# One opening block for two queues, and the last 128 columns for two other engines

## The reference, cut to what matters

```
h = concatenate([meta, x])
for i in range(2):
    a = rmsnorm(h, g[i][0])
    m = retention_mixer(a, ...) if i == 0 else rglru_mixer(a, ...)
    h = h + rmsnorm(m, g[i][1])
    f = conv_ffn(rmsnorm(h, g[i][2]), ...)
    h = h + rmsnorm(f, g[i][3])
return h[:, 16:]
```

## Time and profile before

| what | value |
|---|---|
| median of three runs | 696.47 us (696.41 to 696.52) |
| profiled execution | 696.7 us |
| its span, first to last instruction | 694.9 us |
| TensorE matmul busy | 688.1 us, 99% |
| VectorE busy | 618.9 us, 89% |
| ScalarE busy | 522.3 us, 75% |
| GpSimd busy | 25.2 us, 4% |
| memory read | 129.23 MB |

### The profile page before, as it was taken

One profiled execution on the slowest core, in us unless ns is written; L12 is line 12 of the kernel. 1 busy time (PEld: TensorE's weight loads), 2 busy tenths in 40 slices (PEclk: granted clock), 3 DMA queues, 4 the chain that ended last, 5 costly groups with the idle time before them and its releaser, 6 DMA issues.

```text
span 694.9 us, 15951 instructions
## 1 busy us (share of the span) xinstructions
PE 688.1 (99%) x6471; PEld 579.0 (83%) x6471; DVE 618.9 (89%) x868; ACT 522.3 (75%) x851; POOL 25.2 (4%) x26
## 2 busy tenths in 40 slices
PE   9999999999999999999999999999999999999997
PEld 7888888888999888888889998888888888884454
DVE  6989898978989799998998889999999999999533
ACT  7477867767755888987888677999878888897441
POOL 0002010100110000000003000000000000000000
PEclk9999999999999999999999999999999999999999
DMA  9875656462643455655589941110545656566821
GB/s 345 325 256 155 246 147 252 139 216 105 220 206 121 154 213 191 232 203 199 202 331 384 354 148 62 62 61 1 182 166 199 237 195 224 199 232 220 256 41 61
DMA packets 48635, 134.51 MB, mean 194 GB/s; under 512 B 30784, under 2 KB 31296, under 8 KB 33344
## 3 DMA queue, kind: packets, MB, share of 16 engines
q1 hardware_dynamic: 48288, 133.39, 54.8%
q10 hardware_dynamic: 288, 0.31, 0.1%
HBM read 129.23 MB, written 1.05 MB: 187 GB/s over the span
## 4 chain that ended last, share of the span: by engine, by line
PE 96%; DVE 2%; DMA 1%; issue 1%; ACT 0%; POOLq 0%; DVEq 0%; SPq 0%; ACTq 0%
PE ps L1894 25%; PE ps L1895 25%; PE ps L1896 25%; PE ps L2397 3%; PE ps L2395 3%; PE ps L2396 3%; PE ps L2329 1%; PE ps L1926 1%; PE ps L1947 1%; PE ps L1927 1%; PE ps L2042 1%; PE ps L2049 1%; PE ps L2044 1%; DMA stage<-in_chunks 1%; PE ps L2145 1%
## 5 line engine op out<-in xcount | busy, mean ns | idle before, releaser
L1894 PE MATMUL ps<-a_hi,w_hi 128*128 128x272 f16 (+1 forms) x1008 | 279.2, 277 | 0.2 <-DVE w_lo L1097 0.2
L1895 PE MATMUL ps<-a_lo,w_hi 128*128 128x272 f16 (+1 forms) x1008 | 279.1, 277 | 0.0
L1896 PE MATMUL ps<-a_hi,w_lo 128*128 128x272 f16 (+1 forms) x1008 | 279.1, 277 | 0.0
L1097 DVE SCALAR_TENSOR_TENSOR w_lo<-stage,w_hi 128x1024 f16<-128x1024 f32 x205 | 247.4, 1234 | 20.6 <-ACT w_hi L566 20.2
L566 ACT ACTIVATE w_hi<-stage 128x1024 f16<-128x1024 f32 x205 | 207.8, 1046 | 49.8 <-PE ps L2397 18.3
L1894 PEld LDWEIGHTS ps<-a_hi,w_hi 128*128 128x128 f16 x1008 | 98.6, 98 | 16.8 <-DVE w_lo L1097 0.5
L1896 PEld LDWEIGHTS ps<-a_hi,w_lo 128*128 128x128 f16 x1008 | 98.6, 98 | 16.1
L1895 PEld LDWEIGHTS ps<-a_lo,w_hi 128*128 128x128 f16 x1008 | 98.6, 98 | 16.0
L1894 PE MATMUL ps<-y_hi,w_hi 128*128 128x272 f16 (+3 forms) x496 | 106.1, 242 | 0.0
L1895 PE MATMUL ps<-y_lo,w_hi 128*128 128x272 f16 (+3 forms) x496 | 106.0, 242 | 0.0
L1896 PE MATMUL ps<-y_hi,w_lo 128*128 128x272 f16 (+3 forms) x496 | 106.0, 242 | 0.0
(11 more groups left out here) (320 smaller groups left out, 1074.9 us busy)
## 6 DMA issues: line engine op xcount, KB each, us to landing
stage<-in_chunks SPq DMA_DIRECT2D x118, 1024.0 KB
work<-work SPq DMA_DIRECT2D x96, 32.0 KB, 2.1
stage<-in_chunks SPq DMA_DIRECT2D x6, 256.0 KB
decay_all<-in_decay SPq DMA_DIRECT2D x1, 1056.0 KB, 11.9
out<-sq SPq DMA_DIRECT2D x4, 256.0 KB, 2.0
hT<-in_tokens SPq DMA_DIRECT2D x3, 272.0 KB, 5.5
stage<-in_chunks SPq DMA_DIRECT2D x1, 512.0 KB
mT<-in_gains SPq DMA_DIRECT2D x1, 512.0 KB, 6.7
```

The costliest lines, as they stand in the source:

```text
L1097: dve.scalar_tensor_tensor(out=part(1, c, q), in0=flat(stage, c, q), scalar=W_SCALE, in1=part(0, c, q), op0=ALU.mult, op1=ALU.subtract).th ...
L1894: pe.matmul(o, w_h, x_h, start=start, stop=False)
L1895: pe.matmul(o, w_h, x_l, start=False, stop=False)
L1896: return pe.matmul(o, w_l, x_h, start=False, stop=stop)
```

## The change: what it does

The opening: row 0 of the first chunk (512 columns), the 64 gain columns and token tile 0 (272 columns) now lie side by side in memory and in one SBUF region. Each partition has 848 columns of them, 424 KB in all. Partitions 0 to 63 are brought by SP's queue as its first transfer, partitions 64 to 127 by ACT's queue as its first. VectorE and ScalarE both wait for both halves (`x_landed[0]` at 32). SP's other transfers, and token tile 1 on ACT's queue, keep their order. The rotary table is put over the place where row 0 lay, so its transfer now waits until `w_lo` of row 0 has been made (`even_low`).

The end: for token tile 1, VectorE's second run of line 1809 covers 384 columns. The other 128 are scaled by ScalarE (a copy with the root as its scale, in place), once the root is made (`fin_root`), and GpSimd then adds `h_rows` (`fin_pool`). SyncE waits for `fin_pool` too ahead of the last transfer.

```diff
+OPENING = CW + 8 * DT + T
...
-        hT_all = sb("hT", [P, 8 * DT + DT * T])
-        hT = hT_all[:, 8 * DT:].rearrange("p (a b) -> p a b", b=T)
+        rope_first = sb("rope_first", [P, 2 * T - CW + OPENING + (DT - 1) * T])
+        rope_sb = rope_first[:, 0:2 * T].rearrange("p (a b) -> p a b", b=T)
+        hT_all = rope_first[:, 2 * T - CW:]
+        first_row = hT_all[:, 0:CW]
+        hT = hT_all[:, CW + 8 * DT:].rearrange("p (a b) -> p a b", b=T)
...
+        POOL_COLS = slice(2 * BANK - P, 2 * BANK)
...
             first_chunk = chunks[0:2 * P, :].rearrange("r n -> (r n)")
-            for k0, count in FIRST_ROWS:
+            sp.dma_start(hT_all[0:P // 2, 0:OPENING],
+                         tokens[0:P // 2 * OPENING].rearrange("(p n) -> p n", p=P // 2)).then_inc(x_landed[0], 16)
+            for k0, count in FIRST_ROWS[1:]:
...
                 if c == 1:
-                    sp.dma_start(rope_sb[:], rope).then_inc(table_landed, 16)
+                    sp.wait_ge(even_low, 1)
+                    sp.dma_start(rope_sb, rope).then_inc(table_landed, 16)
...
             for b in range(4):
                 sp.wait_ge(fin_out, b + 1)
+                if b == 3:
+                    sp.wait_ge(fin_pool, 1)
...
                     if dt < KC - 2:
-                        if dt in row_landed:
+                        if dt == 0:
+                            act.wait_ge(x_landed[0], 32)
+                        elif dt in row_landed:
                             act.wait_ge(row_landed[dt], 32)
...
-                        act.activation(w_hi[0][:, dt, :], stage[0][:, dt, :], ACTF.Copy,
+                        act.activation(w_hi[0][:, dt, :], stage[0][:, dt, :] if dt else first_row, ACTF.Copy,
...
-            for n, (a, b) in enumerate(((0, 8 * DT + T), (8 * DT + T, 8 * DT + 2 * T))):
-                act.dma_start(hT_all[:, a:b], tokens[P * a:P * b].rearrange("(p n) -> p n", p=P)).then_inc(x_landed[n], 16)
+            act.dma_start(hT_all[P // 2:P, 0:OPENING],
+                          tokens[P // 2 * OPENING:P * OPENING].rearrange("(p n) -> p n", p=P // 2)).then_inc(x_landed[0], 16)
+            act.dma_start(hT[:, 1, :], tokens[P * OPENING:P * (OPENING + T)].rearrange("(p n) -> p n",
+                                                                                       p=P)).then_inc(x_landed[1], 16)
...
+            act.wait_ge(fin_m, 5)
+            act.wait_ge(rows_landed, 32 * 16)
+            act.wait_ge(fin_root, 2)
+            act.activation(fin[:, 1, POOL_COLS], fin[:, 1, POOL_COLS], ACTF.Copy,
+                           scale=fin_s[:, 4, 1:2]).then_inc(fin_scaled, 1)
...
-            dve.wait_ge(x_landed[0], 16)
+            dve.wait_ge(x_landed[0], 32)
...
-                link(dve.scalar_tensor_tensor(out=r, in0=t_, scalar=3.0, in1=r0, op0=ALU.subtract, op1=ALU.mult))
+                dve.scalar_tensor_tensor(out=r, in0=t_, scalar=3.0, in1=r0, op0=ALU.subtract,
+                                         op1=ALU.mult).then_inc(fin_root, 1)
+                dve.wait_ge(fin_root, tt + 1)
                 dve.wait_ge(fin_m, n_sum)
                 for half in range(2):
-                    cols = slice(half * BANK, (half + 1) * BANK)
+                    cols = slice(half * BANK, POOL_COLS.start if half and tt else (half + 1) * BANK)
...
+            def final_columns():
+
+                pool.wait_ge(fin_scaled, 1)
+                pool.tensor_tensor(fin[:, 1, POOL_COLS], fin[:, 1, POOL_COLS], h_rows[:, 1, POOL_COLS],
+                                   ALU.add).then_inc(fin_pool, 1)
...
+            final_columns()
```

More of the change, by code:

```diff
@@ L179, in build @@
         ones_sb = sb("ones_sb", [P, P])
-        rope_sb = sb("rope_sb", [P, 2, T])
         decay_all = sb("decay_all", [P, 8 * T])
         decay_sb = decay_all[:, 0:HEADS * DECAY_W].rearrange("p (h j) -> p h j", j=DECAY_W)
-        gains_sb = hT_all[:, 0:8 * DT]
+        gains_sb = hT_all[:, CW:CW + 8 * DT]
         par = sb("par", [P, LRU_PARS])
@@ L333, in build @@
         x_landed = [sem(f"x_landed{j}") for j in range(len(TOKEN_LOADS))]
-        row_landed = {k: sem(f"row_landed{k}") for k in (0, 1, 2, 4, 5)}
+        row_landed = {k: sem(f"row_landed{k}") for k in (1, 2, 4, 5)}
         even_high = sem("even_high")
@@ L367, in build @@
         m_est = sem("m_est")
+        fin_root = sem("fin_root")
+        fin_scaled = sem("fin_scaled")
+        fin_pool = sem("fin_pool")
         rs_made = sem("rs_made")
@@ L480, in load_tokens @@
                 dt, count = TOKEN_LOADS[n]
-                at = P * (8 * DT + dt * T)
+                at = P * (OPENING + (dt - 1) * T)
                 sp.dma_start(hT[:, dt:dt + count, :].rearrange("p a b -> p (a b)"),
@@ L1328, in _ @@
                         dve.wait_ge(even_high, dt // 2 + 1)
-                    dve.scalar_tensor_tensor(out=w_lo[0][:, dt, :], in0=stage[0][:, dt, :], scalar=W_SCALE,
+                    dve.scalar_tensor_tensor(out=w_lo[0][:, dt, :], in0=stage[0][:, dt, :] if dt else first_row, scalar=W_SCALE,
                                              in1=w_hi[0][:, dt, :], op0=ALU.mult,
@@ L2478, in laid_out @@
     pieces = [tokens[:, dt:dt + n].reshape(P, n * T) for dt, n in TOKEN_LOADS]
-    pieces[0] = np.concatenate([columns(inputs["norm_gains"]), pieces[0]], 1)
+    pieces[0] = np.concatenate([inputs["ret_w_in"][0][0:P, 2 * D:2 * D + CW], columns(inputs["norm_gains"]), pieces[0]], 1)
     return {"tokens": np.concatenate([piece.ravel() for piece in pieces]), "gains": inputs["norm_gains"],
```

## The result

The changed kernel took 697.38 us, median of 22 runs (697.07 to 699.55); the kernel before, run beside it, 696.49 us, median of 22 (696.11 to 696.92). The medians differ by 0.9 us, where +0.05 us had been forecast, and 697.38 us is outside the stated range of 696.1 to 697.1 us. The ratio is 1.0019, with a 95% interval of 1.0013 to 1.0024; it takes in every run, so the long ones too, and is nearer to the difference of the means, 1.3 us. Of the 22 runs 16 lie between 697.07 and 697.57 us and six between 698.79 and 699.55 us; the kernel before has no such second group.

What follows compares the result with a forecast made beforehand. TensorE's stream of products was taken to bound the kernel, the change touching only head and tail. Opening -0.06 us and tail +0.11 us gave +0.05 us on the median of 696.47 us: 696.5 us, range 696.1 to 697.1 us.

Steps and rivals of the forecast that it cites:

- What bounds the kernel: Whole kernel: TensorE holds 96% of the chain, a stream of products; the change touches only head and tail.
- Between these I take 4.29 us, 0.10 us sooner: Opening: VectorE starts at 4.29 instead of 4.39 us, of which 0.06 us counts.
- the worst end: Opening: q10 keeps its own pace, its half arrives 0.42 us later, VectorE starts at 4.81 us.
- rival (a): Opening: the halves bring nothing, VectorE still starts at 4.39 us; 696.58 us, chance 14%.
- ScalarE and VectorE start within 0.1 us of each other: Opening: line 1317 and the first line 618 start within 0.1 us of each other, near 4.3 us.
- A late arrival is not softened: Opening: a block 0.42 us late would pass to TensorE in full.
- The tail: End: 128 columns fewer on VectorE, ScalarE's copy and GpSimd's addition added, with the lock; +0.11 us in sum.
- the lock: End: GpSimd's addition and VectorE's line 1809 don't run together, which costs VectorE 0.21 us.
- (b): End: no lock, or GpSimd's turn hinders nobody, tail -0.10 us; 696.3 us, chance 12%.
- (c): End: GpSimd comes too late or misses its turn, tail +0.22 us; 696.6 us, chance 12%.
- Rival (d): Opening: ACT's half takes q10's old pace, VectorE starts at 4.81 us, +0.42 us; 697.0 us, chance 11%.
- Rival (e): Opening: a longer gap leaves TensorE's clock at 1.2 GHz, 2 us lost; 698.5 us, chance 4%.

Runs made afterwards that it cites:

- by_cols: Changed kernel's layout and joint wait, old end, but block split by columns over 128 partitions, one transfer per queue: 696.55 us, ratio 0.9999.
- one_sp: Changed kernel's layout, old end, but the block as one transfer of 128 partitions on SP's queue: 696.86 us, ratio 1.0004.
- sp_two: Changed kernel's layout, old end, but the block as two transfers (512 and 336 columns) of 128 partitions, both on SP's queue: 696.66 us, ratio 1.0002.
- sp_halves: Changed kernel's layout, old end, but both halves of 64 partitions issued on SP's queue: 698.69 us, ratio 1.0033.
- open_only: Changed kernel with the end of the kernel before, so only the opening is changed: 697.24 us, ratio 1.0009.
- tail_only: Changed kernel with the opening of the kernel before, so only the end is changed: 696.71 us, ratio 1.0001.
- tail_no_pool: Old opening and changed end, but without GpSimd's addition; SP waits for ScalarE's copy, last 128 columns lack `h_rows`: 696.44 us, ratio 0.9998.
- halves_cols: Changed opening, old end, but each half of 64 partitions in two transfers (512 and 336 columns), four in all: 699.44 us, ratio 1.0041.
- swapped: Changed opening, old end, halves exchanged: SP brings partitions 64 to 127, ACT 0 to 63: 697.26 us, ratio 1.0016.
- warm26: Changed kernel with 26 instead of 18 products on constants ahead of the stream: 697.50 us, ratio 1.0015.

## Why the prediction was wrong, point by point

**What bounds the kernel: right.** The change touches head and tail only, and what is late at the first line 2009 (line 1979 of before) is late for the whole stream, 0.93 us at 7.09 us and, apart from a wait that only the profile of before has, to the end.

**"Between these I take 4.29 us, 0.10 us sooner": wrong, and this is the step that failed.** VectorE started at 5.32 us. That is beyond even the worst end, 4.81 us. The end was built from the pace of q10, so from bytes over time with the start held fixed. The pace was right: the block took 2.07 us from first to last packet, 2.05 before. What moved was either side of it, and neither was a term of the sum: 0.34 us more until the first packet and 0.57 us more after the last. `by_cols`, with the same bytes, the same layout and the same waits, has neither and starts VectorE at 4.44 us; `one_sp` and `sp_two` on 128 partitions have neither, and `sp_halves` has the first alone. So both are shown to come with the split by partitions, the second only where each queue has one half as one transfer. The second lies between the queues' last packets, over at 4.16 us, and the semaphore, full at 5.22 us. Why 64 partitions are slower to issue and why the increments come late stays open.

The first had no row to be read from: none before the change had a first transfer on fewer than 128 partitions. The argument, "neither has the smaller packets, and the packets are larger", put it at nothing without a reason, where it deserved bounds of its own.

The bound from q10's pace also rests on a wrong reading. By the packet records none of the bytes up to 3.5 us were tile 1's, whose first packet starts at 3.58 us, and from there on q10 carried both; the 168 KB block was through at 3.80 us, not at 3.61 us. And q1's first transfer lost 44 KB (256 to 212 KB), not half a row. Neither slip makes the 0.93 us.

The Trainium skill (DMA: Bandwidth & Descriptors, Rules for kernel authors) advises against two transfers to disjoint halves, since they share the same engines. The halves overlapped for 0.37 of 2.07 us and the bytes were no faster, so on that the trace agrees. It was weighed only as rival (a), 696.58 us, in which the halves bring nothing. They cost 0.75 us.

**ScalarE and VectorE start within 0.1 us of each other: right** (5.24 and 5.32 us), and worthless, as the later of two halves sets both. The third row still waited for its transfer, 0.21 us instead of 0.33: it came only 0.51 us later than before (7.71 against 7.20 us), so it was not what held the stream.

**"A late arrival is not softened", 0.42 us would pass in full: right.** `open_only` was 0.78 us behind at its first `w_lo` product, and its median is 0.75 us longer. The 0.31 us that the pair of profiles shows less from 521 us on are, as told above, a late chunk of weights in the one execution of the kernel before.

**The tail: right in each term.** ScalarE's copy 0.40 us (taken: 0.40), the second line 0.81 us (0.82), the lock 0.20 us (0.21) by `tail_only` against `tail_no_pool`, the end 0.07 us later (0.11). GpSimd started its row at 692.22 us, 0.56 us after the first big instruction's start, where 0.54 was told, and took its turn. Rivals (b) and (c) fall.

The Trainium skill (SBUF — State Buffer, Who interferes with whom) lets a GpSimd instruction that reads SBUF and a VectorE one with two SBUF inputs wait for each other; 809 against 612 ns for the same 384 columns agrees with it.

**Rival (d), 697.0 us, was the nearest** (the short runs of the kernel after lie at 697.07 to 697.57 us): right in sign and place, with 0.42 us for the opening where the profile had 0.93 us, wrong in its cause, and it had 11%. That it lies near is luck.

**Rival (e), the clock: its mechanism exists, its part here is not settled.** In `halves_cols` the clock fell after a standstill of 1.92 us and took 1.6 us, near the 2 us told. The kernel after stood still for 0.98 us (1.41 us without a load, which is how the prediction counted) and its profile shows no fall. Its six long runs, 1.8 us above the others, have the right size, but their mean granted clock is that of the short ones, so a fall like the one in `halves_cols` isn't what made them; a late rise could be. No long run was caught with its trace, and `open_only`, with 1.27 us of standstill, has none in eleven runs, while `sp_halves`, with 0.73 us, has five in eight. The length of the standstill alone does not sort them.

## What to carry to other kernels

Split an early block between two queues by columns over all 128 partitions, not by partitions: the same bytes came 0.7 us sooner. A bound on a transfer needs three terms, until its first packet, its bytes, and from its last packet until its semaphore is full, and in this change the two that are not bytes were the ones that moved. And moving the last columns to an idle engine pays only if it doesn't take its turn at SBUF from the engine that is still at work: 128 columns saved 0.13 us and cost 0.20.

## What the runs showed of the hardware that was not expected

- Issuing a first transfer of 64 partitions took 0.56 to 0.60 us on either queue, one of 128 partitions 0.37 to 0.47 us, whatever the bytes (128 or 212 KB against 136 to 424 KB). What was issued behind the halves was slow too: in the kernel after tile 1 took 0.60 us and row 1 0.89 us, before 0.46 and 0.37 us.
- One transfer with rows of 3392 bytes was slower than the same bytes in two, with rows of 2048 and 1344: 2.64 us from first to last packet in `one_sp`, 2.34 us in `sp_two`, and VectorE 0.39 us later. This is one trace of each, and the halves, with rows of 3392 bytes too, took 1.75 to 2.27 us, so the size of the row isn't shown to be the cause.
- Of two equal halves on two queues one goes nearly alone and the other waits for 0.6 to 0.9 us. Which one is not fixed: ACT's in `open_only`, `swapped` and the kernel after, SP's in `warm26`.
- When the clock rises is not fixed either. In the kernel before it was at 2.4 GHz for its first product at 4.90 us; in `by_cols` the first four products, at 5.04 us, took 0.89 us, 1.2 GHz still, and its stream was 0.49 us behind from 8 us on, though VectorE had started only 0.05 us later.

```profile
5.04 1.09 PE L1989 MATMUL ps<-a_hi,w_hi 128*128 128x272 f16 x4
5.93 0.90 PE L1994 MATMUL ps<-a_lo,w_hi 128*128 128x272 f16 x4
6.67 0.63 PE L1999 MATMUL ps<-a_hi,w_lo 128*128 128x272 f16 x4
```
